# Sums over later keys in short-format passes at the end of a unit (second attention)

## The chip, the cores and the metric

One core of a Trainium2 chip. The time is that of the device from the start to the end of one execution, in microseconds (us).

## The reference

The model runs two blocks one after the other over 256 positions of width 1024: the first with two mixers and two gated networks, the second with a pooling mixer, an MLP, then the attention that the change touches, and another MLP. All is float32. The attention ("stick breaking", 16 heads of 64) computes, with q, k and v given:

```
z = einsum('bhqd,bhkd->bhqk', q_blk, k_blk) * inv_sqrt_d
log1m = where(mask, -softplus(z), 0)                     # mask: key before query
excl = cumsum(log1m, axis=3, reverse=True) - log1m       # sum over the later keys
a = where(mask, exp(log_sigmoid(z) + excl), 0)
out = einsum('bhqk,bhkd->bhqd', a, v_blk)
```

The sum over later keys is a product with a triangle of ones, and, from one block of 128 keys to the one before it, with a square of ones.

## The kernel before, in words

**Weights in two parts.** All weights come in *units* of 1 MB (128 partitions by 2048 values). SyncE loads unit u into one of three raw buffers as soon as VectorE is done with the unit that had it (L476). ScalarE rounds it to the short 4-byte format, the high part (`split_hi`, L297), VectorE subtracts that from the raw values, the low part (`split_lo`, L308). TensorE (PE) then multiplies in three passes: high by high, high by low, low by high (`three`, L595 to L597), all in the short format, which takes one pass of the array; a matmul of two full float32 operands shows in the trace as two records, each with a weight load.

**The second attention** takes 16 units: queries, keys and values (12) and the output (4). Units 0 to 2 are run in halves with the normalisation before it; units 3 to 11 follow in the order of `STICK_UNITS`: k0 is unit 2, v0 3, k1 4, v1 5, q2 6, k2 7, v2 8, q3 9, k3 10, v3 11. A unit is 48 matmuls of 256 columns. Each pair of heads is a *step*, 0 to 7; queries and keys of steps 2j and 2j+1 are in units qj and kj, which VectorE copies out of PSUM when the unit is done (`feat_copy`, L1689); ScalarE copies the values (L1302).

**Where the steps stand.** `STICK_MID` puts step t in the middle of a unit (0 in unit 3, 1 in 4, 2 in 5, 3 in 6, 4 in 8, 5 in 9, 6 in 11), `STICK_END` step 7 at the end of unit 11; steps 8 and 9, which only finish what is open, are between the output's units. On PE, `stick_step(t)` is: the scores of step t (`stick_z`, L1065, L1067: 64-row matmuls in float32), the sums of step t-1 (`stick_cum`, L1077, L1079, L1081: triangle by 256 columns, ones by 128, triangle by 128, for each of two heads, in float32), the weighted values of step t-2 (`stick_av`, L1092, L1094). Before an even step PE waits until queries and keys of its pair are copied (`stick_there`).

**VectorE** in the iteration of unit c with a step t: `stick_weights(t)`, which is the mask and scale of the scores (L1949) and the subtraction of the sums of step t-1 from its scores (L1956); the weight split of unit c+2; the copy of the unit; then `stick_rest(t)`: the low part of the output of step t-2 (L1962) and the softplus of step t (L1967), which the sums need. **ScalarE**: absolute value (L1496), exponential (L1498, with a table load of its own), exponential of the weights of step t-1 (L1503), high part of the output (L1197), logarithm (L1509, with a table load), and then the weight split of unit c+3 (L297). **GpSimd** does nothing in this attention but issue loads of gains. Each engine takes its instructions in the order written out; nothing is planned at run time. The sums' operand `sp` has two buffers.

Of the kernel before, what the change touches and what calls it, by code (L numbers as in the profile page):

```python
# [24 lines left out]
P = 128  # L25
# [57 lines left out]

REGION = 42 * 256
X_ROWS_AFTER = 9
# [17 lines left out]
def build(nc, xT, x_rows, gains, cols, rows, ws, wsT, rel_bias, onehot, line_dram, lines_dram, out):  # L103
    ctx = ExitStack()
    with ctx:
# [26 lines left out]
        mean1 = sb("mean1", [P, P])  # L132
        ones = sb("ones", [P, P])
        ident = sb("ident", [P, P])
        tri = sb("tri", [P, P])
        tmask = sb("tmask", [P, KEYS])
# [14 lines left out]

        region = sb("region", [P, REGION])

        def view(at, *shape):
# [10 lines left out]
        x_in = view(0, DT, T)  # L165
        sd2, rs2 = view(9600, T + 2), view(9900, T + 2)
        uT = view(0, DT, T)
# [17 lines left out]
        rden = view(9240, 2, 4)  # L185
        second = view(10272, 2, 2)
        on = view(9248, 2, T)
        diff_low = view(6400, 2, 2, T)
        stick_low = view(9216, 2, 2, T)
        o_junk = view(9760, 4, P)  # L190
        zs = view(6144, 2, 2, KEYS)
        sp = view(6144 + 4 * KEYS, 2, 2, KEYS)
        eb = view(6144 + 8 * KEYS, 2, KEYS)
        ab = view(6144 + 10 * KEYS, 2, KEYS)

# [31 lines left out]
        rel_landed = sem("rel_landed")  # L227
        consts_set = sem("consts_set")
        eps_set = sem("eps_set")
        warm_set = sem("warm_set")  # L230
# [36 lines left out]
            sem("z_done"), sem("z_masked"), sem("z_abs"), sem("z_exp"), sem("z_log"), sem("sp_ready"))  # L267
        cum_done, logw_ready, w_ready, so_done, so_hi, so_lo = (
            sem("cum_done"), sem("logw_ready"), sem("w_ready"), sem("so_done"), sem("so_hi"), sem("so_lo"))

# [214 lines left out]
        def _(pool):  # L485
            pool.memset(warm[:, :], 0.0).then_inc(warm_set, 1)
            pool.memset(mean1[:, :], 1.0 / D).then_inc(consts_set, 1)
            pool.memset(ones[:, :], 1.0).then_inc(consts_set, 1)
            pool.memset(ident[:, :], 0.0).then_inc(consts_set, 1)
            pool.memset(tri[:, :], 1.0).then_inc(consts_set, 1)  # L490
            pool.memset(tmask[:, :], 0.0).then_inc(consts_set, 1)
# [3 lines left out]

            pool.affine_select(out=tri[:, :], in_=tri[:, :], compare_op=ALU.is_ge, fill=0.0, base=0,
                               pattern=[[-1, P]], channel_multiplier=1).then_inc(consts_set, 1)
# [88 lines left out]
            pool.dma_start(kv_gain, gains[ROW_KV_NORM:ROW_KV_NORM + 1, :].broadcast_to([P, D])).then_inc(kv_landed, 16)  # L586
            load_gains(J_STICK)
            load_gains(J_MLP1, count=1)


        @block.tensor
        def _(pe):
# [466 lines left out]
            def stick_z(t):  # L1059
# [9 lines left out]
                mm.then_inc(z_done, 1)  # L1069

            def stick_cum(t):

                pe.wait_ge(sp_ready, t + 1)
                if t:
                    pe.wait_ge(logw_ready, t)
                for e in range(2):
                    pe.matmul(acc[:, 2 + e, 0:2 * P], tri[:, :], sp[:, t % 2, e, 0:2 * P],  # L1077
                              start=True, stop=False, skip_group_check=True)
                    pe.matmul(acc[:, 2 + e, P:2 * P], ones[:, :], sp[:, t % 2, e, 2 * P:3 * P],  # L1079
                              start=False, stop=True, skip_group_check=True)  # L1080
                    mm = pe.matmul(acc[:, 2 + e, 2 * P:3 * P], tri[:, :], sp[:, t % 2, e, 2 * P:3 * P],  # L1081
                                   start=False, stop=True, skip_group_check=True)
                mm.then_inc(cum_done, 1)
# [14 lines left out]
            def stick_step(t):  # L1098

                if t < DT:  # L1100
                    stick_z(t)
                if 1 <= t <= DT:
                    stick_cum(t - 1)
                if t >= 2:
                    stick_av(t - 2)
# [18 lines left out]
            def stick_unit(c, half):  # L1124
# [13 lines left out]
                else:  # L1138
                    if half == 0:
                        pe.wait_ge(sv_ready, 2 * j)  # L1140
                    if c < 11:
                        token_part(u, 2, half, range(DT), b_hi, b_lo)
                    elif half == 0:
                        token_part(u, 2, 0, ks, b_hi, b_lo)
                    else:
                        token_part(u, 2, 0, ks, b_hi, b_lo)
                        token_part(u, 2, 1, range(DT), b_hi, b_lo)

# [7 lines left out]

            stick_first(U_STICK)
            for c in range(3, 12):
                if c == 3:
                    pe.wait_ge(sq_ready, 2)  # L1160
                stick_unit(c, 0)
                if c in STICK_MID:
                    stick_there(STICK_MID[c])
                    stick_step(STICK_MID[c])
                stick_unit(c, 1)
                if c in STICK_END:
                    stick_there(STICK_END[c])
                    stick_step(STICK_END[c])
# [25 lines left out]
        def _(act):  # L1194
# [110 lines left out]
            act.wait_ge(eps_set, 1)  # L1305
            act.activation(table[:, :], eps[:, :], ACT.Copy)
            start()

# [229 lines left out]
        def _(dve):  # L1538
# [403 lines left out]

            def stick_weights(t):

                if t < DT:
                    dve.wait_ge(z_done, t + 1)
                    if t >= 2:
                        dve.wait_ge(w_ready, t - 1)
                    dve.scalar_tensor_tensor(out=zs[:, t % 2, :, :], in0=acc[:, 0:2, 0:KEYS], scalar=QK_SCALE,  # L1949
                                             in1=tmask[:, :].unsqueeze(1).broadcast_to([P, 2, KEYS]),  # L1950
                                             op0=ALU.mult, op1=ALU.add).then_inc(z_masked, 1)
                if 1 <= t <= DT:
                    dve.wait_ge(cum_done, t)
# [3 lines left out]

            def stick_rest(t):

                if t >= 2:  # L1960
                    dve.wait_ge(so_hi, t - 1)
                    dve.tensor_tensor(o_lo_t[:, t - 2, :], stick_out(t - 2), o_hi_t[:, t - 2, :].bitcast(F32),  # L1962
                                      ALU.subtract).then_inc(so_lo, 1)
                if t < DT:
                    dve.wait_ge(z_log, t + 1)
                    dve.wait_ge(z_masked, t + 1)
                    dve.scalar_tensor_tensor(out=sp[:, t % 2, :, :], in0=zs[:, t % 2, :, :], scalar=0.0, in1=eb,  # L1967
                                             op0=ALU.max, op1=ALU.add).then_inc(sp_ready, 1)

            feat_sum(wk[:, 0:2, :], stick_low[:, 0, :, :], s_low, 1, qT[:, 0:2, :], sq_ready)  # L1970
# [3 lines left out]
            for c in range(3, 12):  # L1974
                kind, j = STICK_UNITS[c]
                u = U_STICK + c
                if c in STICK_MID:
                    stick_weights(STICK_MID[c])
                if c == 3:
                    split_lo(dve, U_STICK + 4)  # L1980
                split_lo(dve, u - 1 + CUT)
                if kind == "q":
                    feat_copy(u, 0, qT[:, 2 * j:2 * j + 2, :], sq_ready)
                elif kind == "k":
                    feat_copy(u, 1, kT[:, 2 * j:2 * j + 2, :], sk_ready)
                if c in STICK_MID:
                    stick_rest(STICK_MID[c])
            stick_weights(7)
            split_lo(dve, U_STICK + 11 + CUT)
            stick_rest(7)  # L1990
            stick_weights(8)
            stick_rest(8)
            split_lo(dve, U_STICK + 12 + CUT)
            stick_weights(9)
            stick_rest(9)
            junction(J_STICK)
# [94 lines left out]
```

## Time and profile before

| | us |
|---|---|
| median of 3 runs | 1103.06 (1102.76 to 1104.4) |
| profiled execution | 1102.57 |
| its span, first to last instruction | 1100.7 |
| PE busy | 1066.9 (97%) |
| VectorE busy | 757.6 (69%) |
| ScalarE busy | 634.5 (58%) |
| GpSimd busy | 115.8 (11%) |

The second attention lies between about 796 and 905 us of the span. In the trace PE is the engine of matmuls, PEld its weight loads, DVE VectorE, ACT ScalarE, POOL GpSimd, SP SyncE. "region" is one large buffer of which most tiles are views, `acc` and `wk` are the two halves of PSUM. An arrow in brackets names what ended an idle time.

### The profile page before, as it was taken

Reading aid. Unit: us, or ns where it says so; the run is one execution under the profiler, and the core shown is the slowest. Engines: PE = TensorE matmul, PEld = TensorE weight load, DVE = VectorE, ACT = ScalarE, POOL = GpSimd, SP = SyncE. Lnnn points to the kernel's source line nnn. Section 1 sums busy time; section 2 is a strip of 40 time slices with the busy share of each in tenths; the row PEclk is TensorE's granted clock in tenths of the full one; section 3 lists DMA queues with packets and bytes.
Section 4 is the critical chain, followed back from the end, with each engine's and each line's share of the span. In section 5 each row is a group of like instructions: output and inputs, shape, how many; then the busy total and the mean of one; then the engine's idle time right before and its main releaser. Section 6 shows DMA issues by size and latency. Waiting matters only on the chain.

```text
span 1100.7 us, 15695 instructions
## 1 busy us (share of the span) xinstructions
PE 1066.9 (97%) x6390; PEld 939.1 (85%) x6390; DVE 757.6 (69%) x893; ACT 634.5 (58%) x849; POOL 115.8 (11%) x115
## 2 busy tenths in 40 slices
PE   9999999999989998999998999999999999999997
PEld 8978888887989887888887888888899988888886
DVE  6878777667766787867668865656675658665654
ACT  7656765656555666656566543435577776453532
POOL 0001332120000046221210000000000000000000
PEclk9999999999989999999999999999999999999999
DMA  9836775554525456565553656464354334646451
GB/s 341 324 115 230 249 249 195 188 192 153 191 79 190 138 188 229 170 214 181 184 178 107 213 195 222 159 224 158 144 198 146 124 115 172 215 169 214 168 191 38
DMA packets 31142, 202.21 MB, mean 184 GB/s; under 512 B 3640, under 2 KB 3808, under 8 KB 8544
## 3 DMA queue, kind: packets, MB, share of 16 engines
q1 hardware_dynamic: 28032, 189.16, 48.9%
q0 software_dynamic: 3040, 12.07, 3.3%
q8 instruction: 50, 0.82, 0.3%
q14 instruction: 20, 0.16, 0.0%
HBM read 200.15 MB, written 2.63 MB: 184 GB/s over the span
## 4 chain that ended last, share of the span: by engine, by line
PE 77%; DVE 12%; issue 4%; ACT 4%; POOL 3%; DMA 1%; SPq 0%; DVEq 0%; ACTq 0%; POOLq 0%
PE wk L619 19%; PE wk L649 11%; PE acc L595 8%; PE acc L596 8%; PE acc L597 8%; PE wk L595 4%; PE wk L597 4%; PE wk L596 4%; DVE w_lo L308 4%; PE wk L640 1%; DVE x L1587 1%; DVE region L1603 1%; DVE region L1791 1%; DVE w_lo L319 1%; PE acc L640 1%
## 5 line engine op out<-in xcount | busy, mean ns | idle before, releaser
L308 DVE TENSOR_TENSOR w_lo<-raw,w_hi 128x2048 fp32r<-128x2048 f32 x164 | 375.0, 2290 | 60.8 <-ACT w_hi L297 53.6
L297 ACT ACTIVATE w_hi<-raw 128x2048 fp32r<-128x2048 f32 x173 | 329.4, 1908 | 9.2 <-DMA raw<-ws 6.6
L619 PE MATMUL wk<-a_hl,w_hi 128*128 128x512 f32 x1024 | 243.8, 390 | 4.5 <-DVE region L1781 4.4
L619 PEld LDWEIGHTS wk<-a_hl,w_hi 128*128 128x128 f32 x1024 | 190.5, 188 | 44.0 <-DVE region L1781 5.5
L595 PE MATMUL acc<-w_hi,b_hl 128*128 128x512 f32 x432 | 169.0, 391 | 1.5 <-DVE w_lo L308 1.5
L596 PE MATMUL acc<-w_lo,b_hl 128*128 128x512 f32 x432 | 168.6, 390 | 0.0
L597 PE MATMUL acc<-w_hi,b_hl 128*128 128x512 f32 x432 | 168.1, 389 | 0.0
L649 PEld LDWEIGHTS wk<-a_hl,w_lo 128*128 128x128 f32 x1216 | 155.1, 191 | 5.1
L649 PE MATMUL wk<-a_hl,w_lo 128*128 128x256 f32 x1216 | 158.0, 283 | 0.0
L1472 ACT ACTIVATE region<-wk 128x512 f32<-128x512 f32 x30 | 17.9, 597 | 161.3 <-PE wk L649 161.3
L595 PEld LDWEIGHTS acc<-w_hi,b_hl 128*128 128x128 f32 x432 | 81.3, 188 | 17.9 <-issue 2.3
L597 PEld LDWEIGHTS acc<-w_hi,b_hl 128*128 128x128 f32 x432 | 81.1, 188 | 17.2
L596 PEld LDWEIGHTS acc<-w_lo,b_hl 128*128 128x128 f32 x432 | 81.3, 188 | 15.1
L1791 DVE SCALAR_TENSOR_TENSOR region<-region,prm 128x256 f32<-128x256 f32 x176 | 79.0, 490 | 18.9 <-ACT region L1375 17.3
L1921 DVE TENSOR_TENSOR region<-wk,region 128x512 f32<-128x512 f32 x30 | 20.7, 690 | 91.8 <-ACT region L1472 91.8
L1365 ACT ACTIVATE region<-wk 128x512 f32<-128x512 f32 x42 | 24.9, 592 | 75.9 <-PE wk L649 75.9
L349 POOL TENSOR_TENSOR region<-region 128x512 f32<-128x512 f32 x20 | 49.5, 2477 | 176.9 <-ACT region L1382 176.9
L511 POOL DMA_DIRECT2D gain<-gains x13 | 7.3, 562 | 458.5 <-DVE region L1603 448.0
L595 PE MATMUL wk<-a_hl,w_hi 128*128 128x256 f32 x192 | 55.2, 288 | 0.0
L1781 DVE TENSOR_TENSOR region<-wk,region 128x512 f32<-128x512 f32 x42 | 28.8, 686 | 37.4 <-ACT region L1365 37.4
L597 PE MATMUL wk<-a_hl,w_lo 128*128 128x256 f32 x192 | 54.3, 283 | 0.0
L596 PE MATMUL wk<-a_hl,w_hi 128*128 128x256 f32 x192 | 54.3, 283 | 0.0
(256 smaller groups left out, 1616.3 us busy)
## 6 DMA issues: line engine op xcount, KB each, us to landing
raw<-ws SPq DMA_DIRECT2D x173, 1024.0 KB, 4.9
gain<-gains POOLq DMA_DIRECT2D x13, 512.0 KB, 4.8
raw<-ws SPq DMA_DIRECT2D x8, 256.0 KB, 6.3
region<-rows SPq DMA_DIRECT2D x1, 1664.0 KB, 9.8
lines_dram<-line_dram POOLq DMA_DIRECT2D x1, 1536.0 KB, 8.3
bias<-gains POOLq DMA_DIRECT2D x3, 512.0 KB, 8.1
region<-xT SPq DMA_DIRECT2D x4, 256.0 KB, 4.9
x<-x_rows SPq DMA_DIRECT2D x1, 1024.0 KB, 7.0
```

What stands on the lines that cost most here:

```text
L297: act.activation(w_hi[:, u % HIGH, :], raw[:, u % RAW, :], ACT.Copy).then_inc(hi_ready, 1)
L308: dve.tensor_tensor(low_of(u), raw[:, u % RAW, :], w_hi[:, u % HIGH, :].bitcast(F32), ALU.subtract).then_inc(lo_ready, 1)
L349: eng.tensor_tensor(hf[:, p:p + 2, :], gl[:, p:p + 2, :], cv[:, p:p + 2, 1, :], ALU.mult)\
L595: pe.matmul(o, still, moving, start=first, stop=False, skip_group_check=True)
L596: pe.matmul(o, still, moving_lo, start=False, stop=False, skip_group_check=True)
L597: return pe.matmul(o, still_lo, moving, start=False, stop=last, skip_group_check=True)
L619: pe.matmul(banks[:, m, :], wh[:, k, m * P:(m + 1) * P], a_hl[:, k, :, :].rearrange("p e t -> p (e t)"), start=k == 0, stop=False, skip_gr ...
L640: pe.matmul(banks[:, m, :].rearrange("p (e t) -> p e t", e=2)[:, :, c], wh[:, k, m * P:(m + 1) * P], x[:, k, :, c], start=h == 0 and k == ...
L649: mm = pe.matmul(banks[:, m, T:2 * T], wl[:, k, m * P:(m + 1) * P], hi[:, k, :], start=False, stop=k == DT - 1, skip_group_check=True)
L1365: act.activation(ffn_low[:, a, :, :], ffn_banks(n, i, a)[:, :, T:2 * T], ACT.Copy).then_inc(s["low"], 1)
L1781: dve.tensor_tensor(hb[:, p + a, :, 2:HW], ffn_banks(n, i, a)[:, :, 0:T], ffn_low[:, a, :, :], ALU.add)\
L1791: dve.scalar_tensor_tensor(out=cv[:, p + a, q, :], in0=hb[:, p + a, q, tap:tap + T], scalar=prm[:, bass.ds(col, 1)], in1=cv[:, p + a, q, : ...
```

## The change

For the steps below `SPLIT_SUMS` = 6 the sums are taken in the short format: VectorE copies the softplus into `sp_hi` (rounded), GpSimd subtracts it from `sp` into `sp_lo`, and PE multiplies the triangle by each part (384 columns at once) and the ones by each part's last 128 columns, for two heads: eight matmuls (`stick_cum_parts`). These sums no longer stand in the middle of the unit but behind its second half (in unit 11 behind the first half of the tokens). The sums of steps 6 and 7 stay as they were. On VectorE the mask (`stick_masked`) stays ahead of the weight split, the subtraction of the sums (`stick_weights`) and the low part of the output stand behind it, ahead of the unit's copy. `sp` has one buffer, so a softplus waits for GpSimd's subtraction of the step before. ScalarE's order in the attention is untouched. The constants `ones` and `tri` are made in a scratch place by GpSimd and copied to the short format by ScalarE at the start. Some views in the large buffer have new places.

```diff
@@ -81,7 +81,9 @@
 STICK_END = {11: 7}
 LN_DONE = 11
-REGION = 42 * 256
+SPLIT_SUMS = 6
+
+REGION = 9984
 X_ROWS_AFTER = 9
 PREWARM = 30
...
@@ -183,15 +187,15 @@
         nmx = view(9224, 2, 4)
         den = view(9232, 2, 4)
         rden = view(9240, 2, 4)
-        second = view(10272, 2, 2)
-        on = view(9248, 2, T)
+        second = view(9248, 2, 2)
+        on = view(9252, 2, T)
         diff_low = view(6400, 2, 2, T)
-        stick_low = view(9216, 2, 2, T)
-        o_junk = view(9760, 4, P)
+        stick_low = view(6144, 2, 2, T)
+        o_junk = on.rearrange("p e (n t) -> p (e n) t", n=2)
         zs = view(6144, 2, 2, KEYS)
-        sp = view(6144 + 4 * KEYS, 2, 2, KEYS)
-        eb = view(6144 + 8 * KEYS, 2, KEYS)
-        ab = view(6144 + 10 * KEYS, 2, KEYS)
+        sp = view(6144 + 4 * KEYS, 2, KEYS)
+        eb = view(6144 + 6 * KEYS, 2, KEYS)
+        ab = view(6144 + 8 * KEYS, 2, KEYS)
         HW = T + 2
         hb = region[:, 0:4 * 2 * HW].rearrange("p (s q t) -> p s q t", s=4, q=2)
...
@@ -585,6 +590,11 @@
             pool.wait_ge(xn_ready, turn(J_POOL, 1, 1))
             pool.dma_start(kv_gain, gains[ROW_KV_NORM:ROW_KV_NORM + 1, :].broadcast_to([P, D])).then_inc(kv_landed, 16)
             load_gains(J_STICK)
+            for t in range(SPLIT_SUMS):
+                pool.wait_ge(sphi_ready, t + 1)
+                if t:
+                    pool.wait_ge(cum_done, t)
+                pool.tensor_tensor(sp_lo[:, :, :], sp, sp_hi[:, :, :].bitcast(F32), ALU.subtract).then_inc(splo_ready, 1)
             load_gains(J_MLP1, count=1)
@@ -1068,17 +1078,33 @@
                                    start=True, stop=True, skip_group_check=True)
                 mm.then_inc(z_done, 1)
+            def stick_cum_parts(t):
+
+                for there, part in ((sphi_ready, sp_hi), (splo_ready, sp_lo)):
+                    pe.wait_ge(there, t + 1)
+                    if t and part is sp_hi:
+                        pe.wait_ge(logw_ready, t)
+                    for e in range(2):
+                        pe.matmul(acc[:, 2 + e, 0:3 * P], tri[:, :], part[:, e, :],
+                                  start=part is sp_hi, stop=False, skip_group_check=True)
+                    for e in range(2):
+                        mm = pe.matmul(acc[:, 2 + e, P:2 * P], ones[:, :], part[:, e, 2 * P:3 * P],
+                                       start=False, stop=part is sp_lo, skip_group_check=True)
+                mm.then_inc(cum_done, 1)
+
             def stick_cum(t):
-
+                if t < SPLIT_SUMS:
+                    stick_cum_parts(t)
+                    return
                 pe.wait_ge(sp_ready, t + 1)
                 if t:
                     pe.wait_ge(logw_ready, t)
                 for e in range(2):
-                    pe.matmul(acc[:, 2 + e, 0:2 * P], tri[:, :], sp[:, t % 2, e, 0:2 * P],
+                    pe.matmul(acc[:, 2 + e, 0:2 * P], tri[:, :].bitcast(F32), sp[:, e, 0:2 * P],
                               start=True, stop=False, skip_group_check=True)
-                    pe.matmul(acc[:, 2 + e, P:2 * P], ones[:, :], sp[:, t % 2, e, 2 * P:3 * P],
+                    pe.matmul(acc[:, 2 + e, P:2 * P], ones[:, :].bitcast(F32), sp[:, e, 2 * P:3 * P],
                               start=False, stop=True, skip_group_check=True)
-                    mm = pe.matmul(acc[:, 2 + e, 2 * P:3 * P], tri[:, :], sp[:, t % 2, e, 2 * P:3 * P],
+                    mm = pe.matmul(acc[:, 2 + e, 2 * P:3 * P], tri[:, :].bitcast(F32), sp[:, e, 2 * P:3 * P],
                                    start=False, stop=True, skip_group_check=True)
                 mm.then_inc(cum_done, 1)
@@ -1099,7 +1125,7 @@
                 if t < DT:
                     stick_z(t)
-                if 1 <= t <= DT:
+                if SPLIT_SUMS < t <= DT:
                     stick_cum(t - 1)
                 if t >= 2:
                     stick_av(t - 2)
...
@@ -1155,6 +1182,7 @@
                     pe.wait_ge(sv_ready, 2 * ((t - 2) // 2 + 1))
             stick_first(U_STICK)
+            pe.wait_ge(sums_set, 2)
             for c in range(3, 12):
                 if c == 3:
                     pe.wait_ge(sq_ready, 2)
@@ -1163,6 +1191,8 @@
                     stick_there(STICK_MID[c])
                     stick_step(STICK_MID[c])
                 stick_unit(c, 1)
+                if c in STICK_MID and STICK_MID[c] and c < 11:
+                    stick_cum(STICK_MID[c] - 1)
                 if c in STICK_END:
                     stick_there(STICK_END[c])
                     stick_step(STICK_END[c])
@@ -1304,6 +1334,9 @@
             act.wait_ge(eps_set, 1)
             act.activation(table[:, :], eps[:, :], ACT.Copy)
+            act.wait_ge(consts_set, 9)
+            hi_of(ones[:, :], ones_made, sums_set)
+            hi_of(tri[:, :], tri_made, sums_set)
             start()
@@ -1940,7 +1973,7 @@
             junction(J_MLP0)
-            def stick_weights(t):
+            def stick_masked(t):
                 if t < DT:
                     dve.wait_ge(z_done, t + 1)
@@ -1949,23 +1982,34 @@
                     dve.scalar_tensor_tensor(out=zs[:, t % 2, :, :], in0=acc[:, 0:2, 0:KEYS], scalar=QK_SCALE,
                                              in1=tmask[:, :].unsqueeze(1).broadcast_to([P, 2, KEYS]),
                                              op0=ALU.mult, op1=ALU.add).then_inc(z_masked, 1)
+
+            def stick_weights(t):
+
                 if 1 <= t <= DT:
                     dve.wait_ge(cum_done, t)
                     dve.wait_ge(z_masked, t)
                     z = zs[:, (t - 1) % 2, :, :]
                     dve.tensor_tensor(z, z, acc[:, 2:4, 0:KEYS], ALU.subtract).then_inc(logw_ready, 1)
-            def stick_rest(t):
+            def stick_low_part(t):
                 if t >= 2:
                     dve.wait_ge(so_hi, t - 1)
                     dve.tensor_tensor(o_lo_t[:, t - 2, :], stick_out(t - 2), o_hi_t[:, t - 2, :].bitcast(F32),
                                       ALU.subtract).then_inc(so_lo, 1)
+
+            def stick_soft(t):
+
                 if t < DT:
                     dve.wait_ge(z_log, t + 1)
                     dve.wait_ge(z_masked, t + 1)
-                    dve.scalar_tensor_tensor(out=sp[:, t % 2, :, :], in0=zs[:, t % 2, :, :], scalar=0.0, in1=eb,
+                    if t and t <= SPLIT_SUMS:
+                        dve.wait_ge(splo_ready, t)
+                    dve.scalar_tensor_tensor(out=sp, in0=zs[:, t % 2, :, :], scalar=0.0, in1=eb,
                                              op0=ALU.max, op1=ALU.add).then_inc(sp_ready, 1)
+                if t < SPLIT_SUMS:
+                    dve.wait_ge(sp_ready, t + 1)
+                    dve.tensor_copy(sp_hi[:, :, :], sp).then_inc(sphi_ready, 1)
             feat_sum(wk[:, 0:2, :], stick_low[:, 0, :, :], s_low, 1, qT[:, 0:2, :], sq_ready)
             split_lo(dve, U_STICK + 3)
@@ -1975,24 +2019,28 @@
                 kind, j = STICK_UNITS[c]
                 u = U_STICK + c
                 if c in STICK_MID:
-                    stick_weights(STICK_MID[c])
+                    stick_masked(STICK_MID[c])
                 if c == 3:
                     split_lo(dve, U_STICK + 4)
                 split_lo(dve, u - 1 + CUT)
+                if c in STICK_MID:
+                    stick_weights(STICK_MID[c])
+                    stick_low_part(STICK_MID[c])
                 if kind == "q":
                     feat_copy(u, 0, qT[:, 2 * j:2 * j + 2, :], sq_ready)
                 elif kind == "k":
                     feat_copy(u, 1, kT[:, 2 * j:2 * j + 2, :], sk_ready)
                 if c in STICK_MID:
-                    stick_rest(STICK_MID[c])
+                    stick_soft(STICK_MID[c])
+            stick_masked(7)
             stick_weights(7)
             split_lo(dve, U_STICK + 11 + CUT)
-            stick_rest(7)
+            stick_low_part(7)
+            stick_soft(7)
             stick_weights(8)
-            stick_rest(8)
+            stick_low_part(8)
             split_lo(dve, U_STICK + 12 + CUT)
-            stick_weights(9)
-            stick_rest(9)
+            stick_low_part(9)
             junction(J_STICK)
             mlp_phase(1, U_MLP1, J_STICK)
             junction(J_MLP1)
```

## Rows read from the trace of the kernel before

**Rows 1.** The page: busy time by engine; the chain that ended last, by engine.
```profile
PE 1066.9 (97%) x6390; PEld 939.1 (85%) x6390; DVE 757.6 (69%) x893; ACT 634.5 (58%) x849; POOL 115.8 (11%) x115
PE 77%; DVE 12%; issue 4%; ACT 4%; POOL 3%; DMA 1%; SPq 0%; DVEq 0%; ACTq 0%; POOLq 0%
```

**Rows 2.** The chain of waits, 795 to 915: start us, us, what.
```profile
816.52 0.12 PE wk L595
...
852.50 0.64 PE acc L1065 x4
...
853.36 0.63 PE acc L1077 x2
853.99 0.22 PE acc L1079 x2
...
855.31 0.59 PE wk L1092 x4
...
856.12 0.32 PE wk L595
...
888.33 0.23 PE wk L596
```

**Rows 3.** Timeline of VectorE: start us, us, engine, line, operation [idle before it].
```profile
844.51 0.41 DVE L1962 TENSOR_TENSOR o_lo_t<-wk,o_hi_t 128x256 fp32r<-128x256 f32 x1
...
847.08 2.29 DVE L308 TENSOR_TENSOR w_lo<-raw,w_hi 128x2048 fp32r<-128x2048 f32 x1 [0.84 <-ACT w_hi L297]
849.66 0.69 DVE L1689 COPY region<-wk 128x512 f32<-128x512 f32 x1 [0.29 <-PE wk L597]
...
855.35 0.95 DVE L1956 TENSOR_TENSOR region<-region,acc 128x768 f32<-128x768 f32 x1 [0.97 <-PE acc L1081]
```

**Rows 4.** Timeline of ScalarE, step 4.
```profile
857.31 0.83 ACT L1503 ACTIVATE region<-region 128x768 f32<-128x768 f32 x1
...
858.43 1.28 ACT L1509 ACT_TABLE_LOAD   x1
859.72 0.85 ACT L1509 ACTIVATE region<-region 128x768 f32<-128x768 f32 x1
860.47 1.90 ACT L297 ACTIVATE w_hi<-raw 128x2048 fp32r<-128x2048 f32 x1
```

**Rows 5.** The chain of waits around step 6.
```profile
876.87 0.97 DVE region L1949
...
884.05 0.97 DVE region L1967
885.07 0.70 PE acc L1077 x2
```

**Rows 6.** GpSimd's subtractions (min/median/max ns), and both engines at 420 us.
```profile
L352 POOL TENSOR_TENSOR b_hl<-region,b_hl x20: 1291/1300/1303, 111.1 to 559.9; 128x512 fp32r<-128x512 f32 x20
...
L581 POOL TENSOR_TENSOR region<-region,ident x8: 453/600/2499, 418.5 to 424.1; 128x128 f32<-128x128 f32 x8
...
420.86 2.50 POOL L581 TENSOR_TENSOR region<-region,ident 128x128 f32<-128x128 f32 x1
...
420.50 2.55 DVE L308 TENSOR_TENSOR w_lo<-raw,w_hi 128x2048 fp32r<-128x2048 f32 x1
...
422.97 0.68 DVE L1781 TENSOR_TENSOR region<-acc,region 128x512 f32<-128x512 f32 x1
```

**Rows 7.** Idle PE (in total, times, longest), and stretches with busy times and granted clock.
```profile
PE wk L619 <- DVE region L1781: 4.4, 4, 2.7
PE acc L921 <- DVE region L1859: 4.1, 1, 4.1
...
314.00:316.00 2.00, 1.94 (x9) 1.72 (x10) 1.79 (x6) 0.95 (x2) 0.00 (x0) 0.50 0.93 377
...
318.00:320.00 2.00, 2.00 (x13) 1.84 (x15) 0.52 (x1) 0.00 (x0) 0.00 (x0) 0.55 0.00 0
```

**Rows 8.** Timeline of ScalarE, the start of the kernel.
```profile
4.67 0.91 ACT L1197 ACTIVATE a_hl<-region,prm 128x256 fp32r<-128x256 f32 x2 [2.37 <-DMA region<-xT]
```

More of the change, by code:

```diff
@@ L132, in build @@
         mean1 = sb("mean1", [P, P])
-        ones = sb("ones", [P, P])
+        ones = sb("ones", [P, P], F32R)
         ident = sb("ident", [P, P])
-        tri = sb("tri", [P, P])
+        tri = sb("tri", [P, P], F32R)
         tmask = sb("tmask", [P, KEYS])
@@ L152, in build @@
         region = sb("region", [P, REGION])
+        sp_hi, sp_lo = sb("sp_hi", [P, 2, KEYS], F32R), sb("sp_lo", [P, 2, KEYS], F32R)
         def view(at, *shape):
@@ L165, in build @@
         x_in = view(0, DT, T)
-        sd2, rs2 = view(9600, T + 2), view(9900, T + 2)
+        sd2, rs2 = view(9000, T + 2), view(9260, T + 2)
+        ones_made, tri_made = view(9600, P), view(9600 + P, P)
         uT = view(0, DT, T)
@@ L228, in build @@
         consts_set = sem("consts_set")
+        sums_set = sem("sums_set")
         eps_set = sem("eps_set")
@@ L267, in build @@
             sem("z_done"), sem("z_masked"), sem("z_abs"), sem("z_exp"), sem("z_log"), sem("sp_ready"))
-        cum_done, logw_ready, w_ready, so_done, so_hi, so_lo = (
-            sem("cum_done"), sem("logw_ready"), sem("w_ready"), sem("so_done"), sem("so_hi"), sem("so_lo"))
+        sphi_ready, splo_ready, cum_done, logw_ready, w_ready, so_done, so_hi, so_lo = (
+            sem("sphi_ready"), sem("splo_ready"), sem("cum_done"), sem("logw_ready"), sem("w_ready"), sem("so_done"), sem("so_hi"), sem("so_lo"))
         band_step, band_ready, pool_mapped, pz_ready = (
@@ L487, in _ @@
             pool.memset(mean1[:, :], 1.0 / D).then_inc(consts_set, 1)
-            pool.memset(ones[:, :], 1.0).then_inc(consts_set, 1)
+            pool.memset(ones_made, 1.0).then_inc(consts_set, 1)
             pool.memset(ident[:, :], 0.0).then_inc(consts_set, 1)
-            pool.memset(tri[:, :], 1.0).then_inc(consts_set, 1)
+            pool.memset(tri_made, 1.0).then_inc(consts_set, 1)
             pool.memset(tmask[:, :], 0.0).then_inc(consts_set, 1)
@@ L494, in _ @@
                                pattern=[[-1, P]], channel_multiplier=1).then_inc(consts_set, 1)
[L496 removed]
+            pool.affine_select(out=tri_made, in_=tri_made, compare_op=ALU.is_ge, fill=0.0, base=0,
                                pattern=[[-1, P]], channel_multiplier=1).then_inc(consts_set, 1)
@@ L1165, in _ @@
                 stick_unit(c, 1)
+                if c in STICK_MID and STICK_MID[c] and c < 11:
+                    stick_cum(STICK_MID[c] - 1)
                 if c in STICK_END:
```

## The prediction, as it was recorded

> **What bounds the kernel now.** I read the page first: the matmul engine is busy 97% of the span, and the chain that ended last runs over it for 77%, over VectorE for 12% and over ScalarE for 4% [rows 1]. So a shorter PE pays, if the other two engines keep up. Second, the chain of waits inside the second attention [rows 2]: in step 4 PE spends 0.86 us on the scores (852.50 to 853.36), 1.95 us on the sums over later keys (to 855.31) and 0.81 on the weighted values (to 856.12). Matmuls of 256 columns of the short format follow each other every 0.12 us (the first behind another shape 0.32), of 512 every 0.23 us; a pair of records of the long format of 128 columns takes 0.22 us. Third, the timelines of VectorE and ScalarE for a step [rows 3, 4]: what stands on the two engines between two sums. Here the reader is to see that they have little slack: the copy of unit 7 (keys 4 to 5) ends at 850.35, and the scores of step 4, which need it, begin at 852.50. Last, the stretch around step 6: the softplus of step 6 ends at 885.02 and PE's sums start at 885.07 [rows 5]; there the chain is already on VectorE and ScalarE, not on PE.
>
> **PE's share.** A step's sums are now four matmuls of 384 columns (between the 256's 0.12 and the 512's 0.23: 0.174) and four of 128 (at most 0.12; their columns alone are half of a 0.11 record; I take 0.11, since a weight load goes with each): 1.14 us for 1.95, bounds 0.92 to 1.18 [rows 2]. Six times 0.81 is 4.9 us, if nothing else were late.
>
> **The loop that is made longer.** Now the sums of step t-1 stand at the end of the unit. From their end: subtraction from the scores 0.95 [rows 3]; exponential, with the high part of the output, until the table load of the logarithm 1.12 (857.31 to 858.43); load and logarithm 2.14 [rows 4]; softplus 0.97 [rows 5]; and new: the copy to the high part on VectorE. The trace has no copy from memory to memory; the copy of 512 columns from PSUM takes 0.69, and every VectorE row of 768 columns 0.95 to 0.97 [rows 3, 5], so 0.95, bounds 0 and 0.97. With 0.03 to 0.06 per handoff the high part is there 6.3 us after the sums. Then new on GpSimd: the subtraction, 1.30 us for 512 columns and 0.45 for 128 at the least, a line that gives 1.85 for 768 (bounds 1.30 and 4.1, the latter when it has to stand behind a 2.29 VectorE subtraction) [rows 6]. The low part is there after 8.3 us. (The Trainium skill, VectorE: DVE Perf Modes, Mode 2×_2P, says that a copy from memory to memory moves two 4-byte values per cycle, which would make the copy about 0.55 us, an estimate by that page, and the high part would be there after 5.9; no row here shows such a copy, and what a shorter one would do is rival (b).) PE needs it after scores, values, 0.2 us of change of shape, 48 matmuls (5.76) and the high pass, 0.86 + 0.81 + 0.2 + 5.76 + 0.57 = 8.2 us: late by nothing to 0.2.
>
> What decides is VectorE and its shared port. A subtraction of GpSimd that started while VectorE's weight split ran took 2.50 us for 0.45, and the split, which began while another one of GpSimd's ran, took 2.55 for 2.29 [rows 6]: each waits for the other. After the copy VectorE does the masked scores of the next step (0.97; one operand in PSUM, and such a row took its 0.68 while GpSimd ran), then the split of weights (2.29), which must wait for GpSimd's 1.85. Only behind it stands the next subtraction from the scores. Loop: 6.3 + 1.9 (GpSimd, the mask beside it) + 2.3 = 10.5 us, against 8.8 for a unit of PE. Before, the split stood behind the subtraction and beside PE's half unit. So where steps stand in neighbouring units (1 to 3, 4 and 5) the loop adds lateness.
>
> **Walk in times of the trace before.** (In brackets before: for units 5, 6, 8 and 9 the end of the values in the chain of waits, 856.12 for unit 8 [rows 2], with 0.2 and 24 matmuls of 0.12 behind.) Step 0 is as before, with the mask of step 1 0.8 us late behind the copy. Unit 4: 824.1 (824.7); VectorE, busy with the split until 825.0, subtracts only to 825.9, softplus ends at 830.0, GpSimd at 832.9. Unit 5: PE would be at the low pass at 832.3, waits 0.6: 833.5 (834.3). Unit 6: the values of step 3 wait 0.75 us for the low output of the step before (its subtraction of 0.41 [rows 3] stands behind the late exponential), and the low pass for GpSimd to 843.4: 844.0 (843.9). The gain is gone here. Split until 845.7, subtraction to 846.7, logarithm to 850.1, softplus and copy to 852.0, then the split of unit 9 to 854.3 (before 849.4), the copy of unit 7 to 854.9 (before 850.35). PE ends unit 7 and half of unit 8 at 852.65 and waits **2.3 us** for that copy before the scores of step 4, which end at 855.8 (853.36). Unit 8: 860.8 (859.2). Unit 9: 869.7 (868.8). The same again: subtraction held by the split until 871.4, logarithm to 875.75, softplus and copy to 877.7, ScalarE's split (1.90 behind the logarithm, [rows 4]) to 877.55, VectorE's split of unit 12 to 880.0, copy of unit 10 to 880.6. PE is there at 876.9 and waits **3.7 us**. Scores of step 6 end at 881.5 (876.85): +4.7. From there before took 8.2 us to the sums of step 6 (876.87 to 885.07, [rows 5]) on a chain that the sums of step 5 did not hold. Now these stand 0.8 (values) + 0.2 + 1.44 + 1.14 behind the scores, at 885.1, and the rest of the chain (0.95 + 1.12 + 2.14 + 0.96 and handoffs, 5.4) behind them: 890.5 (885.1), **+5.4 us**. These last sums and all after them are in the old order, so the shift stays to the end.
>
> **What costs nothing.** The two constants on ScalarE at the start, 128 columns each, need GpSimd's constants, there long before ScalarE's first piece at 4.67, ahead of which it idled 2.37 us for a DMA [rows 8]; without cover 0.6 us at most. The layout moves no wait of another stage. SyncE's loads wait for VectorE's splits, which come up to 5 us later against two units of lead; uncovered, a load would add what it is late, and nothing shows it near that.
>
> **Sum.** Profiled execution 1102.57 (span 1100.7 and 1.9 around it) + 5.4 = 1108.0; it stands 0.5 under the median 1103.06, so 1108.5 as a median.
>
> **Rivals.**
> (a) The clock falls. PE idled 4.1 us before the transposes at 314, and its granted clock was 0.50 in 314 to 316 and 0.55 in 318 to 320, so that it came back at about 319.8; an idle of 2.7 us left it at full [rows 7]. My 3.7 us lies between. At 1.2 instead of 2.4 GHz for 5.7 us, 2.9 us of work are lost: 1111.4. The engine's wait of 2.3 us should not do it.
> (b) GpSimd gets the port first. In units 7 and 10 the copy and ScalarE's split end within 0.2 us of each other. If the copy is short, GpSimd starts and the weight split of VectorE with the unit's copy behind it come up to 1.85 us later; the shorter copy gives 0.4 back in each step. Scores of step 6 at 882.2 against PE at 877.2: 5 us idle, +6.8, 1109.9, and with the clock 1112.9. By the rule of the Trainium skill named above, this case is the likelier one.
> (c) The same short copy, but the split wins the port: both waits shrink (1.0 to 2.1 and 2.1 to 3.4 us), 1106.5.
> (d) The port costs next to nothing (the turns fall so that the split never stands behind GpSimd). Then units 5 to 9 end 1.5 to 2.8 us earlier, but unit 10's copy still comes 2.3 us late, and the 0.5 us of the sums of step 5 is lost: within 0.3 us of now, 1103.0.
> (e) The other side: faster. Place: VectorE's copies of units 7 and 10. If they came when PE wants them, PE's 4.9 us would stay except for step 6's 1.3: 1099.5 to 1102. It decides from a loop under 8.8 us, 1.7 shorter than mine. For it speaks PE's 77% of the chain; against it, that the logarithm's 2.14 and exponential are already there in the rows.
>
> **Chances.** Forecast 0.35; (a) 0.15; (b) 0.20; (c) 0.13; (d) 0.10; (e) 0.07. Slower by over 0.2% (2.2 us, about what this kernel's measurement can tell): all but (d) and (e), 0.83; same 0.10; faster 0.07. Of these cases (e) and the upper end of (b), with a second fall of the clock in unit 8 (3.8 us idle there), lie outside 1103.2 to 1114. The forecast's own range, by the bounds of copy and GpSimd, is 1106 to 1110.5.
>
> **What would show it.** Sums of a step near 1.14 us. GpSimd's subtraction near 1.85, or longer by what VectorE holds. PE idle in unit 8 and unit 11 before the scores, released by VectorE's copy of the unit (2.3 and 3.7 us). Softplus of step 6 about 5.4 us after the sums of step 5. The last sums start near 890.5. Wrong it is if PE does not wait for those two copies, or if the split of weights does not come behind GpSimd's subtraction.

## The result and the profile after

The changed kernel takes 1111.49 us (median of 4 runs, 1110.53 to 1112.15) against 1102.96: a ratio of 1.0075, interval 1.0062 to 1.0087. Slower by about 8.5 us. It lies in the range given for all cases (1103.2 to 1114.0), but outside the forecast's own (1106 to 1110.5); the point, 1108.5, was 3 us too low. The case that came true is rival (b), GpSimd ahead of the weight split, together with a fall of the clock; for these two the prediction had 1112.9, 1.4 us too high. All times and ratios leave out three disturbed executions, one of 1485.6 us (short passes at the old place) and two of 1173.6 and 2478.2 us (short passes for step 3 only). The profiled execution took 1111.3 us, span 1109.4. Its lines are new: the scores are L1075 and L1077, the short sums L1088 and L1091, the long ones L1103, the weight split of VectorE L313, the mask L1982, the subtraction of the sums L1992, the softplus L2008, the copy to the high part L2012, GpSimd's subtraction L597.

The page, which answers to [rows 1]: PE is as busy as before, and the chain runs less over it.

```profile
PE 1067.0 (96%) x6366; PEld 939.9 (85%) x6366; DVE 767.3 (69%) x899; ACT 635.3 (57%) x851; POOL 126.8 (11%) x121
PE 74%; DVE 12%; issue 5%; ACT 4%; POOL 3%; DMA 1%; SPq 0%; DVEq 0%; ACTq 0%; POOLq 0%
```

The sums of step 3 in the chain of waits of the changed kernel, answering to [rows 2]: two passes, 859.69 to 860.79, 1.10 us for 1.95.

```profile
859.69 0.35 PE acc L1088 x2
860.04 0.17 PE acc L1091 x2
860.22 0.40 PE acc L1088 x2
860.62 0.17 PE acc L1091 x2
```

VectorE from unit 5 to unit 12, answering to [rows 3]: the copy to the high part takes 0.56 us; the weight splits behind it take 3.29 and 3.83 us for 2.28 (the "port" is what a subtraction of GpSimd and a weight split of VectorE don't use at the same time in these rows; a wait for it shows as a longer instruction, not as idle time); the copy of unit 7 ends at 854.79, that of unit 10 at 881.15.

```profile
831.23 3.29 DVE L313 TENSOR_TENSOR w_lo<-raw,w_hi 128x2048 fp32r<-128x2048 f32 x1
...
849.54 0.56 DVE L2012 CAST sp_hi<-region 128x768 fp32r<-128x768 f32 x1
850.35 3.83 DVE L313 TENSOR_TENSOR w_lo<-raw,w_hi 128x2048 fp32r<-128x2048 f32 x1 [0.25 <-ACT w_hi L302]
854.11 0.68 DVE L1722 COPY region<-wk 128x512 f32<-128x512 f32 x1
855.85 0.96 DVE L1982 SCALAR_TENSOR_TENSOR region<-acc,tmask 128x768 f32<-128x768 f32 x1 [1.07 <-PE acc L1077]
856.73 2.28 DVE L313 TENSOR_TENSOR w_lo<-raw,w_hi 128x2048 fp32r<-128x2048 f32 x1
...
876.76 3.79 DVE L313 TENSOR_TENSOR w_lo<-raw,w_hi 128x2048 fp32r<-128x2048 f32 x1 [0.25 <-ACT w_hi L302]
880.47 0.68 DVE L1722 COPY region<-wk 128x512 f32<-128x512 f32 x1
882.94 0.96 DVE L1982 SCALAR_TENSOR_TENSOR region<-acc,tmask 128x768 f32<-128x768 f32 x1 [1.79 <-PE acc L1077]
...
888.51 0.95 DVE L1992 TENSOR_TENSOR region<-region,acc 128x768 f32<-128x768 f32 x1 [2.42 <-PE acc L1091]
...
892.81 0.96 DVE L2008 SCALAR_TENSOR_TENSOR region<-region 128x768 f32<-128x768 f32 x1 [1.73 <-ACT region L1542]
```

GpSimd, answering to [rows 6]: it starts at 850.18 and 876.59, each time 0.17 us ahead of VectorE's split. The split's end fits a split that does nothing until GpSimd is done: 850.18 + 1.85 = 852.03, and 2.28 behind that is 854.3 (its record ends at 854.18).

```profile
850.18 1.85 POOL L597 TENSOR_TENSOR sp_lo<-region,sp_hi 128x768 fp32r<-128x768 f32 x1 [7.99 <-DVE sp_hi L2012]
...
876.59 1.80 POOL L597 TENSOR_TENSOR sp_lo<-region,sp_hi 128x768 fp32r<-128x768 f32 x1 [8.00 <-DVE sp_hi L2012]
```

PE's rows with an idle time ahead (in brackets): 3.16 us in unit 8, 4.47 in unit 11, 1.57 before the sums of step 6, which answers to [rows 5]. At the first two the profile names no releaser ("issue"); PE starts 0.09 and 0.10 us behind the ends of VectorE's copies, 854.79 and 881.15, and those are what it waits for by the program.

```profile
854.88 0.71 PE L1075 MATMUL acc<-region 64*128 64x256 f32 x4 [3.16 <-issue]
...
881.25 1.23 PE L1075 MATMUL acc<-region 64*128 64x256 f32 x4 [4.47 <-issue]
...
893.82 0.70 PE L1103 MATMUL acc<-region,tri 128*128 128x256 f32 x2 [1.57 <-DVE region L2008]
```

Stretches with busy times and, third from the end, the granted clock, answering to [rows 7]: 0.50 behind the second idle time, that is 1.2 for 2.4 GHz.

```profile
880.00:882.00 2.00, 0.76 (x4) 0.74 (x6) 1.14 (x2) 0.00 (x0) 0.00 (x0) 0.65 0.16 20
882.00:884.00 2.00, 2.00 (x16) 1.34 (x12) 1.06 (x2) 0.07 (x1) 0.00 (x0) 0.50 0.89 365
...
888.00:890.00 2.00, 2.00 (x18) 2.00 (x17) 0.95 (x1) 0.50 (x1) 0.00 (x0) 1.00 1.02 426
```

**Where the time went.** The scores of step 6 start at 881.25 for 875.88 (before), +5.4. From there to the sums of step 6 (893.82 for 885.07) it is 12.6 us for 9.2, +3.4. Together 8.75 of the span's 8.7. The row before:

```profile
875.88 0.71 PE L1065 MATMUL acc<-region 64*128 64x256 f32 x4
```

### The profile page after: what moved, and what is told of

Same layout as the page of the kernel before. It is cut to its first block, busy times and chain, and to the rows that moved or that the text cites. A ratio compares the mean times of both kernels' runs of the same rounds, so it can differ in the third digit from the quotient of the medians.

```text
span 1109.4 us, 15667 instructions
## 1 busy us (share of the span) xinstructions
PE 1067.0 (96%) x6366; PEld 939.9 (85%) x6366; DVE 767.3 (69%) x899; ACT 635.3 (57%) x851; POOL 126.8 (11%) x121
## 4 chain that ended last, share of the span: by engine, by line
PE 74%; DVE 12%; issue 5%; ACT 4%; POOL 3%; DMA 1%; SPq 0%; DVEq 0%; ACTq 0%; POOLq 0%
PE wk L629 19%; PE wk L659 11%; PE acc L605 8%; PE acc L606 8%; PE acc L607 8%; PE wk L605 4%; DVE w_lo L313 4%; PE wk L607 4%; PE wk L606 4%; PE wk L650 1%; DVE x L1620 1%; DVE region L1636 1%; PE acc L650 1%; DVE region L1824 1%; PE acc L795 1%
## 5 line engine op out<-in xcount | busy, mean ns | idle before, releaser
L313 DVE TENSOR_TENSOR w_lo<-raw,w_hi 128x2048 fp32r<-128x2048 f32 x164 | 382.1, 2334 | 61.4 <-ACT w_hi L302 52.8
L1408 ACT ACTIVATE region<-region,prm 128x256 f32<-128x256 f32 x88 | 47.6, 589 | 7.6 <-DVE region L1814 7.6
```

Source lines behind the costliest of these rows:

```text
L313: dve.tensor_tensor(low_of(u), raw[:, u % RAW, :], w_hi[:, u % HIGH, :].bitcast(F32), ALU.subtract).then_inc(lo_ready, 1)
L1408: act.activation(cv[:, p + a, q, :], hb[:, p + a, q, 2:HW], ACT.Identity, scale=w, bias=bb)\
```

## The experiments

Time before in the same session: 1102.71 for copies first, GpSimd's subtraction on VectorE, the move alone and the first warm kernel; 1102.64 for the format alone, both units warm, step 5 in the middle with copies first, and step 3 only; 1102.96 for the other two. Ten kernels ran; unless said otherwise each is the changed kernel with one edit. A ratio is that to the kernel before of the same session, so it can differ by some tenths of a us from a difference of two medians.

### Copies first

```diff
 if kind == "q": feat_copy(...)
 elif kind == "k": feat_copy(...)
 if c in STICK_MID: stick_soft(STICK_MID[c])
+if c not in STICK_MID:
+    split_lo(dve, u - 1 + CUT)      # units 7 and 10, was ahead of the copy
```

> The changed kernel, but in units 7 and 10 (which hold no step) VectorE copies the unit's keys first and splits the weights of unit 9 or 12 behind that; nothing else is touched. Theory (the wait moved: the loss is PE waiting before the scores of steps 4 and 6 for VectorE's copies, which stand behind a weight split that stands behind GpSimd): both idle times of PE vanish or fall under 1 us each (from 3.5 and 4.5), the granted clock stays full, scores of step 6 end near 875.2 instead of 882.9; but the split of unit 12 now delays the mask of step 6 by 2.6 us, so that the sums of step 6 start near 886.3 (893.8 in the changed kernel, 885.1 before): about 1104.2 us. Rival (the loop of VectorE and ScalarE, lengthened by copy and port, is the path in every step; the copies are only where it shows): it gives back at most the 3 us of the clock, 1108 to 1109.

1104.63 us (1102.89 to 1106.17), ratio 1.0015 (1.0006 to 1.0025). Of the two idle times 0.4 us is left, and the scores of step 6 start at 873.39, 2.5 us ahead of before. PE then waits 3.4 us before the sums of step 6, which start at 885.01, where they start before (885.07): that wait only eats up what had been gained. What is still lost comes behind it, where the clock is down: the sums of step 7 start at 894.93 for 893.51. PE's waits in this kernel (in total, times, longest), and a stretch behind the 3.4 us:

```profile
PE acc L1103 <- DVE region L2008: 3.4, 1, 3.4
PE acc L1088 <- POOL sp_lo L597: 0.6, 1, 0.6
PE acc L1075 <- issue: 0.4, 1, 0.4
...
887.00:889.00 2.00, 2.00 (x12) 1.08 (x10) 1.53 (x2) 1.97 (x3) 0.00 (x0) 0.50 0.00 0
```

The theory stands: 6.9 of the 8.5 us hung on the order of four instructions (the price of the clock in the changed kernel, measured further down, is part of them). "The clock stays full" was wrong: it fell behind PE's wait before the sums of step 6, which I had let stand. So was the start of those sums, expected at 886.3.

### GpSimd's subtraction on VectorE

```diff
-pool.tensor_tensor(sp_lo, sp, sp_hi, ALU.subtract)
+dve.tensor_tensor(sp_lo, sp, sp_hi, ALU.subtract)      # behind the copy to sp_hi
```

> The changed kernel, but the low part of the softplus is subtracted by VectorE itself, behind its copy to the high part; GpSimd has no part in it. Theory (the port blocks the weight split for about 1.0 us in units with a step and 1.5 us in units 7 and 10): the splits fall from 3.3 and 3.8 us to 2.28, VectorE gains 1.0 and loses 0.96 per step with neighbours (equal), and gains 0.5 per idle time in units 7 and 10; the low part is there 0.9 us sooner, so PE's waits for it vanish (0.65 us once). With the clock still falling in unit 11: 1110 to 1111, a gain of 0.5 to 1.5 us. Rival (the subtraction is cheap on GpSimd and the port is no matter): VectorE has 0.96 us more in each of six steps and it gets slower, by 1 to 3 us: 1112.5 to 1114.

1109.43 us (1107.88 to 1110.58). Its VectorE in unit 7:

```profile
849.70 0.96 DVE L2009 TENSOR_TENSOR sp_lo<-region,sp_hi 128x768 fp32r<-128x768 f32 x1
850.58 2.29 DVE L313 TENSOR_TENSOR w_lo<-raw,w_hi 128x2048 fp32r<-128x2048 f32 x1
852.78 0.69 DVE L1717 COPY region<-wk 128x512 f32<-128x512 f32 x1
```

0.96 us more work on the busy engine, and 2 us faster (somewhat more than expected): the splits are back at 2.29, the copy of unit 7 ends at 853.47 for 854.79. The port was a real price, of 1 us per step and 1.5 in units 7 and 10. In this profiled execution the clock fell behind both idle times (3.14 and 3.61 us), in the changed kernel's only behind one; so it was faster in spite of the clock.

### The move alone, in float32

```diff
 def stick_cum(t):
-    if t < SPLIT_SUMS:
-        stick_cum_parts(t)
-        return
```

> The changed kernel, but the sums of steps 0 to 5 are taken in float32 as before the change, without copy to a high part and without GpSimd, at the new place (end of the unit) and in the new order on VectorE: the move alone. Theory (order and place cost by themselves, copy and port come on top): VectorE's loop from sums to sums is 8.6 us, under PE's 9.6, so steps in neighbouring units cost nothing; the scores of step 4 wait 0.5 us, those of step 6 1.9 us for the unit's copy, and the sums of step 6 come 1.6 us later behind the late sums of step 5; changes of shape saved give back 1.2: 1105 to 1106.5, no fall of the clock. Rival (the price is all in the conversion and in GpSimd): no slower than before, 1102 to 1103.5.

1105.95 us (1105.78 to 1108.13), as expected. PE waits 2.5 us for copies, 1.6 before the sums of step 6 (in total, times, longest); below them a stretch behind the 2.0 us:

```profile
PE acc L1070 <- issue: 2.5, 2, 2.0
PE acc L1095 <- DVE region L1998: 1.6, 1, 1.6
...
880.00:882.00 2.00, 2.00 (x11) 1.95 (x10) 1.12 (x1) 1.94 (x2) 0.00 (x0) 0.53 0.24 90
```

The move alone costs 3.2 us, without any work of GpSimd; short passes at the new place cost 5.5 more instead of giving 4.9 back. One item of the expectation was wrong: the clock did fall for a while behind the 2.0 us (0.53).

### The format alone, at the old place

Sums in `stick_step` as before, VectorE in its old order, six steps in short passes.

> The changed kernel with the short passes for six steps, but with the sums in the old place (middle of the unit, after the scores of the next step) and VectorE's old order: the format alone. Theory (neighbouring steps have no time for copy and GpSimd's subtraction: 2.5 us from softplus to low part): the low pass waits 1.8, 0.8 and 2.0 us in units 5, 6 and 9 (more at first in unit 4), the price of which eats what the passes save; the copies of units 7 and 10 come 2 us later, the second 0.6 us too late: 1104 to 1104.6, slower than before by 1.1 to 1.7 and faster than the change by 7. Rival (the format is harmless and the place alone costs): PE's 0.8 us per step comes through, 1099 to 1101.

1104.04 us (1103.0 to 1106.41), ratio 1.0014 (1.0005 to 1.0024). The time is the forecast one; no single wait of this kernel is shown, so the causes that the expectation names are argued. The format alone costs about 1.5 us, not 5.5: with the 3.2 us of the move that is 4.7 of the 8.5, and the rest is there only when both halves of the change stand together.

### Warm in unit 11, then in both units

```diff
+if c in (8, 11):                                  # the first try: only 11
+    pe.wait_ge(z_masked, 4 if c == 8 else 6)
+    keep_warm(acc[:, 0, 0:T], 24 if c == 8 else 36)
```

> The changed kernel with 36 matmuls of 256 columns on a constant, written to the bank that the scores of step 6 then overwrite, in the time in which PE idles in unit 11 (4.5 us): PE does not idle, and nothing else is changed. Theory (the fall of the granted clock to 0.50 behind the idle time costs PE work and makes the sums of step 5 late, on which the chain of step 6 hangs): the clock stays at 1.00, the sums of step 6 start 9.8 to 10 us after the start of the scores of step 6 instead of 12.6: 2.5 to 3 us faster than the changed kernel, 1108.5 to 1109. Rival (the chain on VectorE and ScalarE hides it): within 0.5 us of the changed kernel.

1110.10 us (1109.81 to 1111.69): 1.4 faster by the medians, not 3, and with four executions that overlap the changed kernel's (1110.53 to 1112.15) not clear of no gain. In the profiled execution from scores to sums of step 6 it is 9.8 us (882.46 to 892.26) as expected, but the clock had fallen in unit 8, where it had held in the changed kernel's:

```profile
856.00:858.00 2.00, 2.00 (x13) 1.67 (x10) 2.00 (x2) 1.40 (x2) 0.00 (x0) 0.50 0.93 393
```

The idle time ahead was 3.16 us in both. So an idle time of 3.16 us is followed by a fall of the clock in one execution and not in another. The scores of step 6 came 1.2 us later by it (882.46 for 881.25). Hence the second try.

> The changed kernel with 24 matmuls on a constant in the idle time of unit 8 and 36 in that of unit 11, so that PE idles at neither. In the profiled run with 36 in unit 11 alone the clock fell to 0.50 at 856 to 859 us instead, behind the 3.2 us of unit 8. Theory (either idle time can bring the clock down, and the clock's whole price is then gone): clock 1.00 throughout the attention, 1108.4 to 1109, and less spread between runs. Rival (the clock has no price here, what the first try gained was something else): 1110 as with unit 11 alone.

1107.97 us (1107.84 to 1108.41), with no stretch of the attention under 1.00:

```profile
855.00:860.00 5.00, 5.00 (x45) 4.58 (x44) 3.16 (x2) 2.97 (x3) 0.00 (x0) 1.00 0.74 223
...
880.00:885.00 5.00, 4.45 (x39) 3.75 (x37) 3.93 (x4) 1.88 (x2) 0.00 (x0) 1.00 0.65 213
```

Its scores and sums of step 6:

```profile
881.14 0.71 PE L1075 MATMUL acc<-region 64*128 64x256 f32 x4 [0.55 <-issue]
...
890.93 0.70 PE L1103 MATMUL acc<-region,tri 128*128 128x256 f32 x2 [1.56 <-DVE region L2011]
```

The scores start where they do in the changed kernel (881.25), since the copy of unit 10 sets them, and the sums 2.9 us earlier (893.82): that is the price of one fall, and the whole difference of the two profiled spans (1109.4 and 1106.5). By the medians the clock's price is 3.5 us (1111.49 to 1107.97), by the differences to before 3.2; with four executions of each kernel the tenths are not sure, but the two kernels' times don't overlap, and the spread of the runs fell from 1.6 to 0.6 us. The rest, 5.3 us against before, stays with the clock full; it is waits, less what the passes save.

### Copies first, and the sums of step 5 in the middle again

```diff
-SPLIT_SUMS = 6
+SPLIT_SUMS = 5
 # VectorE, unit 11
+if c == 11: stick_weights(6)      # ahead of the weight split
```

> The kernel with copies first in units 7 and 10, and besides the sums of step 5 back in float32 in the middle of unit 11 (five steps in short passes instead of six), with their subtraction on VectorE ahead of the weight split there. Theory (sums at the end of a unit are in the way only of step 6, whose chain they prolong, and of the copies; short passes pay on PE where a step has time for them): the mask of step 6 starts at 875.2 (876.9 before, 876.7 with copies first alone), its sums at 883.3 (885.1 before): 1101 to 1101.7, faster than before by 1.2 to 1.9 us. Rival (the new place costs in every step by VectorE's loop of 9.8 us): it stays at or above the 1104.6 of the kernel with copies first alone.

1100.60 us (1100.23 to 1101.04), ratio 0.9978 (0.9969 to 0.9987): faster than before by 2.0 us by the medians and 2.4 by the ratio, more than expected, and than the change by 10.9. The granted clock stays at 1.00 from 812 to 912. VectorE in unit 11, with mask and subtraction together ahead of the split; PE waits 1.4 us before the sums of step 6, which start at 882.77 (885.07 before):

```profile
874.58 0.95 DVE L1981 SCALAR_TENSOR_TENSOR region<-acc,tmask 128x768 f32<-128x768 f32 x1
875.45 0.94 DVE L1991 TENSOR_TENSOR region<-region,acc 128x768 f32<-128x768 f32 x1
876.31 2.29 DVE L313 TENSOR_TENSOR w_lo<-raw,w_hi 128x2048 fp32r<-128x2048 f32 x1
```

### The same without the short format

> The best kernel so far (copies first in units 7 and 10, sums of step 5 in the middle of unit 11) with the sums of steps 0 to 4 in float32 at the end of their units, without copy, GpSimd and short passes. It tells what the short format is worth there. Theory (format worth 0.8 us on PE in five steps, of which neighbouring steps give half back to waits for the low part): 1 to 2 us slower than the 1100.6 of the kernel with short passes, 1101.6 to 1102.6, about the time of the kernel before. Rival (the whole gain is the order of VectorE and the saved changes of shape): the same time, 1100.3 to 1101.

1102.36 us (1101.53 to 1103.46), ratio to before 0.9994 (0.9985 to 1.0003). So in the best kernel the short format is worth 1.8 us by the medians and 1.3 by the profiled executions (1101.53 and 1100.25), and order and place by themselves nothing that can be told from before. This kernel also has the two constants made at the start and the new places of the views, so these cost nothing that can be told either.

### Only the sums of step 5 in the middle

> The changed kernel with the sums of step 5 back in float32 in the middle of unit 11 and their subtraction ahead of the weight split there; the copies of units 7 and 10 stay behind the splits. Theory (two independent prices): GpSimd does not stand in the way in unit 10 any more, so that the scores of step 6 start 1.5 us earlier, at 879.7, and the sums of step 6 start 9.1 us behind them instead of 12.6 (of which 2.8 were the clock): 888.8 against 893.8, so 1106 to 1107.5; the idle time before step 6 is 3 us, and whether the clock falls there or in unit 8 decides the rest. Rival (only the copies matter): 1109 to 1110.5.

1110.09 us (1108.14 to 1111.64): above the theory's range. In the profiled execution the waits were as it said (2.98 us before the scores of step 6, 3.15 before those of step 4, none before the sums of step 6), but the clock was at 0.50 behind both idle times, as these stretches show:

```profile
855.00:860.00 5.00, 5.00 (x27) 3.98 (x26) 3.15 (x2) 2.74 (x3) 0.00 (x0) 0.50 0.54 203
...
884.00:886.00 2.00, 2.00 (x7) 1.82 (x8) 0.88 (x1) 1.07 (x2) 0.00 (x0) 0.50 0.79 332
```

The rival's number with the theory's waits: this run tells them apart only by its trace. That profiled execution took 1111.42, the fastest of the four 1108.14.

### Short passes for step 3 only, in the old kernel

> The kernel before with short passes for the sums of step 3 only, in the old place (these have unit 7 between softplus and use, 7 us): one copy on VectorE, one subtraction on GpSimd, six pairs of long records fewer on PE. Theory (PE is the path between step 4 and the scores of step 6, so what a step saves there comes through; nothing waits, since GpSimd's 1.85 and the split behind it end 0.8 us ahead of the need): 0.8 us faster than before, 1102.0 to 1102.3. Rival (the split pushed back by GpSimd makes the copy of unit 7 late): no gain or slower.

1101.49 us (1100.72 to 1103.45), ratio 0.9992 (0.9983 to 1.0001): in the expected direction, 0.9 us by the ratio for 0.8, but not clear of no change. VectorE in unit 7: the split waits for the port again (3.83), and the copy ends at 852.76, in time for the scores of step 4, which start at 853.66 with no idle time of PE ahead.

```profile
847.50 0.56 DVE L2007 CAST sp_hi<-region 128x768 fp32r<-128x768 f32 x1
848.32 3.83 DVE L313 TENSOR_TENSOR w_lo<-raw,w_hi 128x2048 fp32r<-128x2048 f32 x1 [0.26 <-ACT w_hi L302]
852.08 0.68 DVE L1717 COPY region<-wk 128x512 f32<-128x512 f32 x1
```

## Why the prediction was right, and where not

**Right: the place and the mechanism.** PE was to wait for VectorE's copies of units 7 and 10, behind a weight split that stands behind GpSimd. Forecast and measured: sums 1.14 and 1.10 us; GpSimd's subtraction 1.85 and 1.85; softplus of step 6 after the sums of step 5 5.4 and 5.3 us (888.51 to 893.77, the subtraction's start to the softplus' end). That copies first took most of the loss away, and that the kernel got faster with more work on VectorE and none on GpSimd, shows it.

**Luck: two numbers.** The scores of step 4 ended at 855.8, as forecast, by two errors of opposite sign. The copy to the high part was done at 850.10 for 852.0, mainly since the loop from one subtraction of the sums to the next was shorter than forecast (9.8 us, 834.45 to 844.26, for 10.5); and the weight split behind it ended 3.8 us after it started, for 2.3. And 1111.49 us is next to the 1111.4 of rival (a), in which the clock falls but the split has the port first, which it had not.

**Wrong: the copy at 0.95 us.** "The trace has no copy from memory to memory ... so 0.95": it took 0.56. The step took the price of rows of 768 columns none of which is a copy. The Trainium skill (VectorE: DVE Perf Modes, Mode 2×_2P) has two 4-byte values per cycle for this form, the estimate by it was 0.55, and the trace agrees. The shorter copy did not make the kernel faster but let GpSimd reach the port ahead of the split, as rival (b) has it: the scores of step 6 started 5.4 us late for 4.7. That is less than half of the way to (b)'s own figures: it had them at 882.2 behind 5.0 us of idle time and in unit 8 3.8 us, against 881.25, 4.47 and 3.16. The chance of 0.20 for (b) was too low for a rule whose conditions (source in memory, an even outer dimension, here 2) this copy meets.

**Wrong: the clock as a rival of its own.** The forecast took 3.7 us of idle time as safe, with a chance of 0.15 for a fall, and said of the 2.3 us in unit 8 that it "should not do it". They were 4.47 and 3.16 us; the clock fell behind the longer one in the change's profiled execution, behind one of 3.14 to 3.16 in unit 8 in three others (the first warm kernel, GpSimd's subtraction on VectorE, step 5 alone), and behind one of 1.95 us in the move alone. The price of one fall, 2.9 us, was right: 2.9 between the profiled executions of the change and of the kernel with both units warm. What was wrong is that the point held no part of it. In the profiled execution, 3.3 us above the forecast's span, the start of the scores of step 6 accounts for 0.7 and the stretch from there to the last sums, 12.6 us for 9.9, for 2.7.

**Small misses.** The low pass was to wait 0.6 us in unit 5: it did not, since GpSimd was done at 832.37 for 832.9; in unit 6 it waited 0.65 for about 1.0. Most of both comes from the shorter copy. The values in unit 6 were to wait 0.75 us for a low part: they start 0.15 us behind its end (837.14 and 836.99), 0.2 us behind the scores.

**The other side.** Rival (e) had PE's 4.9 us through, except for step 6's 1.3, if the copies came in time. With copies first and step 5 out of the way it came to 2.0 to 2.4 us: 1.4 us are still lost before the sums of step 6, on the chain of VectorE and ScalarE that bounds step 6 in the kernel before too.

**Open.** How much of the 5.5 us between the move alone and the change is the port and how much the clock in single units: the clock's 3 to 3.5 were measured in the change (not in the move alone, where it fell too), the port's 2 only through a kernel in which the clock fell as well. Which waits make up the 1.5 us of the format alone. And why at the same idle time the clock falls in one execution and not in another.

## What to carry to other kernels

When an instruction is moved to an engine that shares a port, look at what stands in the queue behind its neighbour on the other engine, and who waits for that: here much of the cost was not in the sums but in a copy two instructions later, and swapping two lines gave back 6.9 of 8.5 us. It was not the port alone: the new place by itself cost 3.2 us, with 2.5 us of waits for the same two copies. A cheaper format pays for the steps that have time for the conversion; here keeping five of six steps and moving the sixth back turned 8.5 us lost into some 2 gained, of which 1.3 to 1.8 are the format's. Price an idle time of a few microseconds of TensorE with the clock behind it, and as a spread, not as a yes or no.

## What the runs showed of the hardware that was not expected

An idle time of PE of 1.95 us, ending at 877.00, was already followed by a granted clock of 0.61 and 0.53 (the move alone, in 878 to 880 and 880 to 882), while one of 3.16 us in unit 8 left it at 1.00 in the change's profiled execution. A weight split of VectorE beside GpSimd's subtraction shows as running all the time (3.29 and 3.83 us; 2.29 with that subtraction on VectorE), so a list of idle times does not find the wait. A kernel with 60 matmuls more that compute nothing needed (both units warm) is 3.5 us faster.
